# Two transformer blocks on one core: x loaded transposed, the first norm's row factor taken into the products, the first two units k-outer

## The reference

```python
def rms_norm(x, g):
    xf = x.astype(jnp.float32)
    r = lax.rsqrt(jnp.mean(xf * xf, axis=-1, keepdims=True) + RMS_EPS)
    return (xf * r).astype(x.dtype) * g
...
        h = rms_norm(x, norm_g[layer])
        proj = h @ w_in[layer]
        dq, dk, dv, dz, nq, nkv, nz, ng = jnp.split(proj, IN_SPLITS, axis=-1)

        dq = rms_norm(dq.reshape(B, T, DIFF_HEADS, 2, DIFF_QK_DIM).transpose(0, 2, 3, 1, 4), diff_q_norm_g[layer])
        dk = rms_norm(dk.reshape(B, T, DIFF_HEADS, 2, DIFF_QK_DIM).transpose(0, 2, 3, 1, 4), diff_k_norm_g[layer])
...
        kc = compress(nkv[0], cmp_pos[layer, 0], cmp_w1[layer, 0], cmp_b1[layer, 0], cmp_w2[layer, 0])
```

## Time and profile before

| | |
|---|---|
| median of 3 runs | 1061.03 us (1060.91 to 1061.03) |
| profiled execution, its span | 1059.3 us |
| TensorE busy | 1049.8 us (99%) |
| VectorE busy | 496.7 us (47%) |
| ScalarE busy | 455.8 us (43%) |
| GpSimd busy | 398.5 us (38%) |
| chain that ended last | TensorE 97%, VectorE 1%, DMA 1%, ScalarE 1% |

### The profile page before, as it was taken

How to read it: one execution, slowest core, us unless ns; L and a number is a source line. 1 busy time by engine, 2 the same in 40 slices (tenths; PEclk the granted TensorE clock), 3 DMA queues, 4 the chain that set the end, 5 groups by cost and what they waited for, 6 DMA issues and landing times.

```text
span 1059.3 us, 14497 instructions
## 1 busy us (share of the span) xinstructions
PE 1049.8 (99%) x5573; PEld 839.1 (79%) x5573; DVE 496.7 (47%) x1047; ACT 455.8 (43%) x794; POOL 398.5 (38%) x300
## 2 busy tenths in 40 slices
PE   9999999999999999999999999999999999999997
PEld 7777897767678876888777888888888888888886
DVE  5754688875752316998587344230000000032444
ACT  6455557676653425233465414342221221233533
POOL 3555520001025334446000255434435354465772
PEclk9999999999999999999999999999999999999999
DMA  9631221201032331332221232323232323323221
GB/s 296 189 117 54 71 80 41 76 16 47 25 120 80 72 118 41 102 98 80 80 80 41 80 103 96 90 79 110 82 116 79 115 83 103 115 80 100 82 97 80
DMA packets 84724, 95.72 MB, mean 90 GB/s; under 512 B 8121, under 2 KB 70930, under 8 KB 84666
## 3 DMA queue, kind: packets, MB, share of 16 engines
q1 hardware_dynamic: 83706, 92.46, 27.9%
q0 software_dynamic: 560, 2.12, 0.6%
q10 hardware_dynamic: 400, 0.35, 0.1%
HBM read 92.80 MB, written 2.12 MB: 90 GB/s over the span
## 4 chain that ended last, share of the span: by engine, by line
PE 97%; DVE 1%; DMA 1%; ACT 1%; issue 0%; ACTq 0%; DVEq 0%
PE bank L1864 59%; PE bank L2177 23%; PE bank L1923 4%; PE bank L1954 3%; PE bank L1995 3%; PE bank L1971 1%; PE bank L2152 1%; PE bank L1815 1%; PE bank L2028 1%; PE bank L1905 1%; DMA PT<-in_onehot 1%; PE bank L1984 0%; PE bank L1947 0%; PE bank L2073 0%; DVE L L1506 0%
## 5 line engine op out<-in xcount | busy, mean ns | idle before, releaser
L1030 POOL TENSOR_TENSOR w_lo<-raw,w_hi 128x512 fp32r<-128x512 f32 (+1 forms) x190 | 266.8, 1434 | 435.1 <-ACT w_hi L1092 422.6
L1864 PE MATMUL bank<-h_hi,w_hi 128*128 128x512 f32 (+1 forms) x560 | 224.4, 401 | 0.3 <-ACT h_hi L1299 0.2
L1864 PE MATMUL bank<-h_hi,w_lo 128*128 128x512 f32 (+1 forms) x560 | 218.7, 390 | 0.0
L1864 PE MATMUL bank<-h_lo,w_hi 128*128 128x512 f32 (+1 forms) x560 | 217.8, 390 | 0.0
L1092 ACT ACTIVATE w_hi<-raw 128x512 fp32r<-128x512 f32 (+3 forms) x94 | 111.3, 1214 | 118.1 <-PE bank L1864 114.5
L1070 POOL TENSOR_TENSOR w_lo<-raw,w_hi 128x512 fp32r<-128x512 f32 x88 | 110.7, 1290 | 133.5 <-ACT w_hi L1337 67.1
L1864 PE MATMUL bank<-w_hi,h_hi 128*128 128x512 f32 (+2 forms) x397 | 145.4, 366 | 0.0
L1864 PE MATMUL bank<-w_hi,h_lo 128*128 128x512 f32 (+2 forms) x397 | 144.5, 364 | 0.0
L1864 PE MATMUL bank<-w_lo,h_hi 128*128 128x512 f32 (+2 forms) x397 | 144.5, 364 | 0.0
L2177 PE MATMUL bank<-h_hi,w_hi 128*128 128x512 f32 x352 | 137.1, 389 | 0.0
L2177 PE MATMUL bank<-h_hi,w_lo 128*128 128x512 f32 x352 | 137.1, 389 | 0.0
(11 more groups left out here) (211 smaller groups left out, 1240.4 us busy)
## 6 DMA issues: line engine op xcount, KB each, us to landing
raw<-in_w_in SPq DMA_DIRECT2D x29, 1024.0 KB, 5.3
raw<-in_w_ffn_gate SPq DMA_DIRECT2D x11, 1024.0 KB, 5.3
raw<-in_w_ffn_up SPq DMA_DIRECT2D x11, 1024.0 KB, 5.3
raw<-in_w_out SPq DMA_DIRECT2D x8, 1024.0 KB, 5.0
raw<-in_w_ffn_down SPq DMA_DIRECT2D x8, 1024.0 KB, 5.0
raw<-in_w_in SPq DMA_DIRECT2D x8, 512.0 KB, 4.5
pool<-in_cmp_w SPq DMA_DIRECT2D x4, 1024.0 KB, 9.1
raw<-in_w_ffn_down SPq DMA_DIRECT2D x4, 768.0 KB, 4.3
```

The source lines that it names most:

```text
L1030: nc.gpsimd.tensor_tensor(w_lo[:, u.n % 2, cols], raw[:, u.n % 2, cols], w_hi[:, u.n % 2, cols].bitcast(F32), ALU.subtract).then_inc(lo_do ...
L1864: ins = mm(bank[t.bank][0:t.m, 0:u.width if u.token else T], stationary, moving, start=first and n == 0, stop=last and n == len(products) ...
```

## The change

**Loads.** x comes transposed from the host (x_t, 8 pieces of 128 columns by 512 tokens), each pair of pieces with the quarter of w that goes with it, for the first two units, diff_q and cmp_kv. All small vectors come as one array of 128 x 95 straight into col, on ScalarE's queue; the lambdas and the distances are two loads on the sync queue. x in its own layout, for the residual, is loaded later, with the second unit of nsa_q.

**The head.** ScalarE takes x_t times the gain as h_hi, without the row's factor. TensorE goes through k outside and the four tiles of the two units inside, over four banks. ScalarE squares x_t and VectorE adds the squares up over k; ahead of k = 6 TensorE adds them over partitions with a matrix of ones, so that each partition holds every token's sum. Root and reciprocal give rbc, the factor for each token along the free axis, and a small copy along partitions.

**Evacuations.** Everything that comes from a product of the first block now needs that factor. VectorE multiplies it in when it takes the bank: (bank x step) x rbc for dq and nq, bank x rbc for dk and kd, for the compression tiles and for z and nz. ScalarE's squares read what VectorE wrote and wait for ve_evac; for dk and kd ScalarE then multiplies the gain in. Tanh of z reads what VectorE wrote too, and a new step of VectorE, z_finish, multiplies. Tiles with tokens on partitions (dv, vd, the gates) get the factor as ScalarE's scale. The gains of q are taken into those of k.

**Moved.** The two products of the bias table go from the start to behind the first 12 products of diff_k, the evacuations of both compression tiles to behind the head, and so ahead of small_arrays on VectorE. The 32 transposes of x and the 20 small loads are gone; 18 products of zeros are left of 22.

The diff, cut to its core:

```diff
-    project(dq_u[:1] + [kv_u] + dk_u[:1], RING4, 4, small_arrays)
...
+    left[4] = left[5] = [("r_root", 2)]
+    emit("head")
+    emit("split", u=order[2], of=order[1])
+    for o in range(0, PIECE * len(head_part), PIECE):
+        emit("high_piece", u=order[2], o=o)
+    for t in head_tiles[:2]:
+        evacuated(t)
+    emit("high_piece", u=order[2], o=PIECE * len(head_part))
+    for t in head_tiles[2:]:
+        evacuated(t)
+    for u in head_units:
+        follow(u)
+    project(dk_u[:1], RING4, 4, small_arrays)
...
+            for q in range(ND // 2):
+                ks = slice(2 * q, 2 * q + 2)
+                sp.dma_start(x_t[:, 2 * q, :], a["x_t"][:, 2 * q, :]).then_inc(xt_in[2 * q], 16)
+                for j, u in enumerate(head_units):
+                    sp.dma_start(slot(raw, j, u)[:, ks, :], u.parts[0][0][:, ks, :]).then_inc(head_in[2 * q + j], 16)
+                sp.dma_start(x_t[:, 2 * q + 1, :], a["x_t"][:, 2 * q + 1, :]).then_inc(xt_in[2 * q + 1], 16)
...
+            def head():
+
+                for q in range(ND // 2):
+                    for k in (2 * q, 2 * q + 1):
+                        sc.wait_ge(xt_in[k], 16)
+                        if k == 0:
+                            sc.wait_ge(cols_in, 16)
+                        act_fn(h_hi[:, k, :], x_t[:, k, :], ACT.Copy, scale=col[:, R_NORM + k:R_NORM + k + 1]).then_inc(h_hi_done, 1)
+                        for j in range(2) if k % 2 == 0 else ():
+                            cols = slice(PIECE * q, PIECE * q + PIECE)
+                            sc.wait_ge(head_in[2 * q + j], 16)
+                            act_fn(w_hi[:, j, cols], raw[:, j, cols], ACT.Copy).then_inc(hi_done, 1)
+                    for k in (2 * q, 2 * q + 1):
+                        if k >= 2:
+                            sc.wait_ge(sq_added, max(k - 2, 1))
+                        act_fn(square_rows[:, k % 2, :], x_t[:, k, :], ACT.Square).then_inc(sq_done, 1)
+                sc.wait_ge(ss_mm, 1)
+                act_fn(rbc[:, :], bank[4][:, :], ACT.Sqrt, scale=1.0 / D, bias=eps).then_inc(r_root, 1)
+                act_fn(st[:, ST_RS:ST_RS + NT], bank[5][:, 0:2 * NT].rearrange("p (i c) -> p i c", c=2)[:, :, 0], ACT.Sqrt,
+                       scale=1.0 / D, bias=eps).then_inc(r_root, 1)
...
-                sc.wait_ge(tile_done, t.done)
-                if kind in NORM + AUX_COPY:
+                if kind in NORM:
                     if t.x_in == 1:
                         sc.wait_ge(setup_done, 1)
+                    sc.wait_ge(ve_evac, t.ve)
                     wait_free(sc, t.ax_waits)
...
+                    x = dests[kind][:, idx, :]
+                    for half in range(2):
+                        from_, rows = slice(DH * half, DH * half + DH), slice(DH * (half ^ idx % 2), DH * (half ^ idx % 2) + DH)
+                        scale = 1.0 / step_value(kind, idx, half) if kind in ("dq", "nq") else 1.0
+                        if idx % 2 or kind == "nq":
+                            ins = act_fn(scratch(t)[rows, :], x[from_, :], ACT.Square, scale=scale)
+                        elif half == 0:
+                            ins = act_fn(scratch(t), x, ACT.Square, scale=scale)
+                    if t.squared:
+                        ins.then_inc(row_squares, 1)
+                        sc.wait_ge(row_squares, t.squared)
+                        ins = act_fn(x, x, ACT.Copy, scale=gains[kind](idx))
+                    ins.then_inc(aux_in, 1)
+                    return
                 if kind in ("z", "nz"):
-                    if kind == "nz" and idx == 0:
-                        sc.wait_ge(norm_done, t.norms)
-                        sc.wait_ge(aux_done, t.auxes)
-                    act_fn(mix(idx + (4 if kind == "nz" else 0)), src, ACT.Tanh, scale=0.5).then_inc(sc_evac, 1)
+                    sc.wait_ge(ve_evac, t.ve)
+                    if t.z > 2:
+                        sc.wait_ge(z_done, t.z - 2)
+                    act_fn(z_tanh[:, t.z % 2, :], mix(idx + (4 if kind == "nz" else 0)), ACT.Tanh, scale=0.5).then_inc(sc_evac, 1)
+                    return
...
+                ve.wait_ge(r_root, 1)
+                v.reciprocal(rbc[:, :], rbc[:, :]).then_inc(r_done, 1)
+                ve.wait_ge(r_root, 2)
+                chain(v.reciprocal(st[:, ST_RR:ST_RR + NT], st[:, ST_RS:ST_RS + NT]))
+                v.tensor_scalar(st[:, ST_SS:ST_SS + NT], st[:, ST_RR:ST_RR + NT], 0.5, None, ALU.mult).then_inc(r_done, 1)
+                ve.wait_ge(r_done, 2)
+                ve.wait_ge(const_in, 16)
 
             def small_arrays():
+                ve.wait_ge(cols_in, 16)
                 ve.wait_ge(small_in, 16 * N_SMALL)
-                ve.wait_ge(col_tr, 2)
-                v.tensor_copy(col[:, ND:NROWS], bank[COL_BANK][:, ND:NROWS]).then_inc(col_done, 1)
-                ve.wait_ge(col_done, 2)
-
-                for r, base in ((R_GNQ, 0), (R_GDQ, 4)):
-                    v.tensor_scalar(st[:, ST_GNQ + base:ST_GNQ + base + 4], const[:, K_STEP + base:K_STEP + base + 4],
-                                    col[:, r:r + 1], -(DH ** -0.5), ALU.mult, ALU.mult)
+
+                v.tensor_scalar(col[:, R_GDK:R_GDK + 1], col[:, R_GDK:R_GDK + 1], col[:, R_GDQ:R_GDQ + 1], None, ALU.mult)
+                v.tensor_scalar(col[:, R_GKC:R_GKC + 3], col[:, R_GKC:R_GKC + 3], col[:, R_GNQ:R_GNQ + 1], None, ALU.mult)
...
                 if kind in NORM:
-                    ve.wait_ge(aux_in, t.x_in)
+                    ve.wait_ge(tile_done, t.done)
                     if kind in ("nq", "kd") and idx == 0:
                         ve.wait_ge(hid_mm, 2)
-                    v.tensor_scalar(dests[kind][:, idx, :], src[:, :], gains[kind](idx), None, ALU.mult).then_inc(ve_evac, 1)
+                    if kind in ("dq", "nq"):
+                        v.scalar_tensor_tensor(dests[kind][:, idx, :], src[:, :], steps_at(kind, idx), rbc[:, :],
+                                               ALU.mult, ALU.mult).then_inc(ve_evac, 1)
+                    else:
+                        v.tensor_tensor(dests[kind][:, idx, :], src[:, :], rbc[:, :], ALU.mult).then_inc(ve_evac, 1)
                 if kind in ("z", "nz"):
                     x = mix(idx + (4 if kind == "nz" else 0))
-                    ve.wait_ge(sc_evac, t.sc)
-                    v.scalar_tensor_tensor(x, x, 1.0, src[:, :], ALU.add, ALU.mult).then_inc(ve_evac, 1)
+                    ve.wait_ge(tile_done, t.done)
+                    if kind == "nz" and idx == 0:
+                        ve.wait_ge(norm_done, t.norms)
+                        ve.wait_ge(aux_done, t.auxes)
+                    v.tensor_tensor(x, src[:, :], rbc[:, :], ALU.mult).then_inc(ve_evac, 1)
...
-                        v.tensor_copy(shifted[0:DH, idx, kv, :], src[half, :])
-                        ins = v.tensor_copy(shifted[DH:P, idx, kv, 0:T - 1], src[half, 1:T])
+                        v.tensor_tensor(shifted[0:DH, idx, kv, :], src[half, :], rbc[half, :], ALU.mult)
+                        ins = v.tensor_tensor(shifted[DH:P, idx, kv, 0:T - 1], src[half, 1:T], rbc[half, 1:T], ALU.mult)
...
-            for n in range(22):
+            for n in range(18):
                 mm(bank[4][:, 0:P], idle_rows, idle_rows, start=True, stop=True)
...
+            def head():
+
+                for k in range(ND):
+                    if k == ND - 2:
+                        pe.wait_ge(ones_done, 1)
+                        pe.wait_ge(sq_added, ND - 1)
+                        mm(bank[4][:, :], ones_all, square_sum, start=True, stop=True)
+                        for i in range(NT):
+                            ins = mm(bank[5][:, 2 * i:2 * i + 2], square_sum[:, P * i:P * i + P], ones_all[:, 0:2],
+                                     start=True, stop=True)
+                        ins.then_inc(ss_mm, 1)
+                    q = k // 2
+                    products = [(n, p) for n in range(4) for p in range(3)]
+                    if k < 2:
+                        products = [(n, p) for p in range(3) for n in range(4)]
+                    for n, p in products:
+                        t, j = head_tiles[n], n // 2
+                        if n == 0 and p < 2:
+                            wait_free(pe, [(h_hi_at, h_lo_at)[p][R_NORM, k]])
+                        if k % 2 == 0 and n % 2 == 0:
+                            if p == 0:
+                                pe.wait_ge(hi_done, 2 * q + j + 1)
+                            if p == 2:
+                                pe.wait_ge(lo_done, 2 * q + j + 1)
+                        w, x = ((w_hi, h_hi), (w_hi, h_lo), (w_lo, h_hi))[p]
+                        ins = mm(bank[t.bank][:, :], slot(w, j, head_units[j])[:, k, t.c0:t.c0 + P], x[:, k, :],
+                                 start=k == 0 and p == 0, stop=k == ND - 1 and p == 2)
+                        if k == ND - 1 and p == 2:
+                            ins.then_inc(tile_done, 1)
+                    if k % 2 and k < ND - 1:
```

(8 more changed lines are left out.)

301 lines of the change are left out of this document (156 added, 145 removed).

## The result

The changed kernel takes **1102.62 us** (median, 1101.38 to 1105.37), beside 1060.97 for the kernel before in the same comparison: 1.0395 times as long, 95% interval 1.038 to 1.041. Slower was forecast, by 31 us; it is 41.6. The forecast of 1092 and its range up to 1100 were too low.

The account below looks back on a forecast made before the run. TensorE, busy 99%, bounds the kernel. Profiled 1059.3 + 25.6 (lag from five waits, head's gain included) + 5.2 (clock) = 1090.1; as median, 1061.0 + 30.8 = 1092 us, range 1082 to 1100.

Parts of the forecast that it names:

- the mechanism: Sums of squares wait for ScalarE's squares, which now wait for VectorE's evacuations, taken in list order.
- the five waits: TensorE idle ahead of the first sums, dk0/dk1, dk2/dk3, nq2/nq3 and kd: 10.2, 7.8, 5.3, 5.0, 2.1 us.
- The late setup_done: First squares wait for VectorE's causal add behind both compression tiles; TensorE waits 10.2 us, ending 5.4 us behind.
- the late reciprocals: Two reciprocals (6.55 us) between the evacuations of a unit's two tiles on VectorE make the other four waits.
- The start at 6.7: First real product on TensorE, forecast at 6.8 us, behind the 18 idle products.
- the new evacuations: VectorE takes banks of dq0 and dq1 at 0.75 us each before ScalarE squares them; likewise in later units.
- the 1.8 us: Head: possible late landing of the packed columns, 380 B rows written by read-modify-write; kept for the range.
- the clock: Granted clock falls in the waits; 1.4 us lost each, 0.3, three in full (4.2), 0.7: together 5.2 us.
- the head: First block ends at 30.4, 4.8 us ahead without waits; VectorE's chain then puts the first sums at 43.4.
- The slow additions: Compression tiles on VectorE: two additions 1.94 us, or 3.71 with GpSimd beside them; the slower kept for the range.
- the attention: 150 to 300 us: eight new VectorE evacuations of z and nz, 6 us, taken at nothing; up to 3 us.
- rival D: Slow additions beside GpSimd, slower return of the clock, VectorE short in the attention: over 1100 us; chance 0.08.

Follow-up runs that it names:

- the first two experiments: Changed kernel with setup_done awaited ahead of dk0's squares: 1094.02 us; separately, with diff_q's and nsa_q's reciprocals behind the next unit's second evacuation: 1081.08 us.
- The filled waits: Changed kernel with idle identity products on TensorE in the waits ahead of four sums (38, 26, 19 and 18 products): 1094.22 us.
- The run with the old way for z: Kernel with setup_done later and reciprocals later (1073.87 us), plus z and nz read from the bank as before, without row factor: 1071.80 us.

## Why the prediction was right and wrong

**Right: the mechanism and the five waits.** The places, the engines and the sizes hold: 10.2, 7.8, 5.3, 5.0 and 2.1 forecast, 10.21, 6.74, 5.34, 5.15 and 2.35 measured, none ahead of dq2/dq3 and nq0/nq1. That the first comes out to the tenth is in part luck: TensorE was ready at 35.2, not 33.2, and the squares were late by the same 2.0. The late setup_done and the late reciprocals are shown by the first two experiments. The start at 6.7 and the new evacuations were as put. The packed columns landed 3.8 us after their issue, and ScalarE's first rounding started at 4.59. (The Trainium skill, DMA: Bandwidth & Descriptors, section Specifications, has pieces under 512 B written by read-modify-write; the 1.8 us that I gave it were not paid.)

**Mis-sized: the clock.** The prediction took 1.4 us for each wait, from the start of the earlier trace rows, and found the first one's loss covered up to 0.3. Behind a wait it was 2.3 to 2.5, and 3.4 behind the first, of which VectorE covered 1.1 (the second wait is 6.74, not 7.8, for that reason). The step that failed was to take one row for the price of every wait, with no bounds. In this kernel it was half of the work done at 1.2 GHz, 4.8 to 6.9 us of it. In all runs the loss behind a wait of 4.7 us or more lies between 1.4 and 4.9 us and doesn't follow the wait's length: 1.4 behind 12.00 us, 3.4 and 4.9 behind 10.2. So 1.4 was the low end of a spread; what sets the place in it no run shows. The fifth, put at 0.7, cost nothing. Sum against the forecast: 3.1 - 1.1 + 3.0 - 0.7 = **4.3 us**. The filled waits show the cause; a loss of 9.5 was expected there from these sizes, and 8.4 came back.

**Mis-sized: the head, 2.0 us.** The first sums came at 45.43, not 43.4. The step that failed is that the sum of squares was put in without VectorE's additions of the squares. Four of the seven took 1.6 to 1.8 us, those beside GpSimd's low pieces, and the others 0.7 (here two of each):

```profile
17.83 3.48 DVE L1434 TENSOR_TENSOR pool<-pool 128x512 f32<-128x512 f32 x2
...
22.56 1.48 DVE L1434 TENSOR_TENSOR pool<-pool 128x512 f32<-128x512 f32 x2
26.82 3.35 DVE L1437 RECIPROCAL rbc<-rbc 128x512 f32<-128x512 f32 x1 [2.79 <-ACT rbc L1121]
```

So the sum of squares waited 0.89 us, its products took 1.9 instead of 1.6, and the reciprocal began at 26.8, not 25.6; the narrow operations behind it took 1.2 instead of 0.4. TensorE, too, came 2.0 late to the sums: diff_k had waited 0.53 us for dq0's bank. The slow additions that the prediction kept for its range are others, those of the compression tiles, and these came as put, at 1.9 for two.

**Wrong in its value: the attention.** It stood at 0, with 3 as its end. It cost 2.3: waits of 1.38, 0.89 and some small ones, 3.1 together where there had been 0.8. The run with the old way for z bears out that they are the new evacuations', and 3 was a fair bound.

Up to the sums of kd the lag is 37.7 us where 30.8 was forecast: 2.0 and 4.3 and some tenths in the waits. The attention adds 2.3. The profiled execution lies 3.0 us under the median, and that of before 1.7: 1.3 more. That fits the clock as well: the four executions took 1101.38, 1101.42, 1103.81 and 1105.37 us at mean granted clocks of 0.983, 0.983, 0.981 and 0.978, and the profile is of the first; of the others no trace was kept. Together 10.5 of the 10.6: all four erred to the same side. The range had stopped at 1100 since it added the bounds of the head and the attention and gave the clock none; its slower return stood in rival D, which had a chance of 0.08 in all.

## What to carry to other kernels

Where an operation is moved off the engine that reads a bank to one that is served in order, follow that engine's whole list: what stands ahead of the moved operation is its price, and here order and waits were worth 39 of 42 us. Price a wait of the busiest engine twice: the idle time, and then half of the work that it does until its clock is back, with bounds (here 1.4 to 4.9 us, whatever the length of the wait); if the wait can't be removed, filling it with idle products is worth a try. And when a wait is taken away, look for the next instruction in the same lists before counting its gain: the 10.2 us taken away left 5.3 more in the next wait, and a move that mended one wait of 6 us made another of 4.7.

## What the runs showed of the hardware

In the waits of 4.7 us and more of this case's runs the clock fell 2.2 to 5.4 us after TensorE fell idle, where the tail of the kernel before had 2, and it came back after 2.9 to 9.9 us of work at 1.2 GHz. Neither goes with the length of the wait. Behind the same first wait of 10.2 us it came back after 6.9 us of work in one kernel and after 9.9 in another. Twice it fell while TensorE was back at work: at 47.5 behind 1.8 us of idle time, in the run with filled waits, and at 143.4 behind 0.57, in the run with the old way for z; another run idled 0.57 us at the same place, and there the clock stayed up. With 2.35 and 2.37 us of idle time it stayed up, with 2.46 it fell. So a wait of about 2 us may or may not cost it.
